# A gated layer of 32 experts: the next chunk's first two products stand between a chunk's turns and its second products, and tokens are gathered token-major two chunks ahead

## What is computed

```python
def moe_ffn(h, w_router, b_router, w1, b1, w2, b2):
    logits = (hf @ w_router + b_router).astype(jnp.float32)
    top_v, top_e = lax.top_k(logits, TOP_K)          # 4 of 32
    gates = jax.nn.softmax(top_v, axis=-1)
    ...
    def expert_block(args):
        xi, e = args
        hc = xi @ w1[e] + b1[e]                       # 1024 -> 2048
        g, u = hc[:, :D_EXPERT], hc[:, D_EXPERT:]
        g = jnp.minimum(g, SWIGLU_LIMIT)
        u = jnp.clip(u, -SWIGLU_LIMIT, SWIGLU_LIMIT)
        hm = (u + 1.0) * (g * jax.nn.sigmoid(SWIGLU_ALPHA * g))
        return hm @ w2[e] + b2[e]                     # 1024 -> 1024
```

## Time and profile before

| | us |
|---|---|
| median of 3 runs (2340.43 to 2341.96) | 2341.57 |
| the profiled execution | 2340.47 |
| its span, first to last instruction | 2338.7 |
| TensorE matmul busy | 2244.8 (96%) |
| VectorE busy | 714.5 (31%) |
| ScalarE busy | 620.8 (27%) |
| bytes moved | 688.71 MB, mean 294 GB/s |

### The profile page before, as it was taken

One profiled execution on the slowest core, in us unless ns is written; L12 is line 12 of the kernel. 1 busy time (PEld: TensorE's weight loads), 2 busy tenths in 40 slices (PEclk: granted clock), 3 DMA queues, 4 the chain that ended last, 5 costly groups with the idle time before them and its releaser, 6 DMA issues.

```text
span 2338.7 us, 36205 instructions
## 1 busy us (share of the span) xinstructions
PE 2244.8 (96%) x13812; PEld 1373.0 (59%) x13813; DVE 714.5 (31%) x1376; ACT 620.8 (27%) x903; POOL 394.1 (17%) x371
## 2 busy tenths in 40 slices
PE   7999999999999999999998999999999999999898
PEld 5887744444444444444446988899998863333333
DVE  4864322222222222222225244312315341111013
ACT  2143111111111111112124671443458011111111
POOL 2000000000000000000003761688586000000000
PEclk9999999999999999999999999999999999999999
DMA  9973399999999999989994533555454475999652
GB/s 359 381 259 110 101 411 418 418 418 418 418 418 418 417 418 418 418 363 380 418 418 167 179 109 108 180 183 180 127 180 117 155 287 216 402 405 396 276 230 84
DMA packets 223487, 688.71 MB, mean 294 GB/s; under 512 B 28330, under 2 KB 117362, under 8 KB 187570
## 3 DMA queue, kind: packets, MB, share of 16 engines
q1 hardware_dynamic: 221776, 685.82, 76.4%
q10 hardware_dynamic: 1490, 1.61, 0.2%
q0 software_dynamic: 144, 0.20, 0.0%
HBM read 686.53 MB, written 1.05 MB: 294 GB/s over the span
## 4 chain that ended last, share of the span: by engine, by line
PE 72%; DMA 11%; SPq 11%; DVE 3%; issue 2%; ACT 1%; POOL 0%; ACTq 0%; DVEq 0%; POOLq 0%
PE PS L1102 17%; PE PS L702 12%; DMA RAW<-in_w_exp_in 10%; PE PS L691 6%; SPq L467 6%; PE PS L1206 6%; PE PS L676 6%; PE PS L1066 4%; PE PS L1217 3%; SPq L489 3%; PE PS L1407 3%; PE PS L1085 2%; PE PS L748 1%; PE PS L1113 1%; SPq L497 1%
## 5 line engine op out<-in xcount | busy, mean ns | idle before, releaser
L1102 PE MATMUL PS<-RAW,Z 128*64 128x512 f32 x3168 | 713.3, 597 | 24.1 <-DMA RAW<-in_w_exp_in 23.2
L409 POOL TENSOR_TENSOR WLO_D<-W,WHI_D 128x512 fp32r<-128x512 f32 x284 | 360.2, 1304 | 1159.6 <-ACT SPARE L1632 965.9
L1102 PEld LDWEIGHTS PS<-RAW,Z 128*64 128x64 f32 x3168 | 213.7, 136 | 454.7 <-issue 376.8
L1206 PE MATMUL PS<-W,Z 128*64 128x512 f32 (+1 forms) x1056 | 212.5, 558 | 10.9 <-DMA W<-in_moe_w 10.2
L702 PE MATMUL PS<-Z,W 128*128 128x256 f32 x768 | 170.1, 382 | 1.5 <-DVE Z L2072 1.5
L405 ACT ACTIVATE WHI_D<-W 128x2048 fp32r<-128x2048 f32 x71 | 135.3, 1908 | 114.0 <-DMA W<-in_ffn_w 42.3
L1206 PEld LDWEIGHTS PS<-W,Z 128*64 128x64 f32 x1056 | 74.5, 137 | 148.9 <-issue 129.6
L702 PEld LDWEIGHTS PS<-Z,W 128*128 128x128 f32 x768 | 146.4, 191 | 23.0 <-DVE Z L2072 1.9
L1066 PE MATMUL PS<-Z 128*128 128x64 f32 x1088 | 125.3, 273 | 0.0
L1066 PEld LDWEIGHTS PS<-Z 128*128 128x128 f32 x1088 | 124.2, 192 | 0.2 <-issue 0.2
L2194 DVE TENSOR_TENSOR Z<-Z,PS 128x1024 f32<-128x1024 f32 x66 | 80.4, 1218 | 126.0 <-PE PS L1085 126.0
(11 more groups left out here) (405 smaller groups left out, 2692.8 us busy)
## 6 DMA issues: line engine op xcount, KB each, us to landing
RAW<-in_w_exp_in SPq DMA_DIRECT2D x256, 1024.0 KB, 19.2
RAW<-in_w_exp_out SPq DMA_DIRECT2D x128, 1024.0 KB, 21.7
W<-in_moe_w SPq DMA_DIRECT2D x128, 704.0 KB, 15.7
W<-in_w_in SPq DMA_DIRECT2D x52, 1024.0 KB, 5.4
W<-in_moe_w SPq DMA_DIRECT2D x40, 1024.0 KB, 15.9
W<-in_ffn_w SPq DMA_DIRECT2D x33, 1024.0 KB, 5.3
W<-in_w_ada SPq DMA_DIRECT2D x24, 1024.0 KB, 14.2
W<-in_w_out SPq DMA_DIRECT2D x12, 1024.0 KB, 5.0
```

Source lines behind the costliest of these rows:

```text
L409: i = eng.tensor_tensor(lo[:, c:c + 512], raw[:, c:c + 512], hi[:, c:c + 512].bitcast(F32), ALU.subtract)
L1102: mm = pe.matmul(ps(bank, 512, 64 * h, 64 * h + 64), x, w[:, c:c + 512], start=first, stop=final, skip_group_check=True)
L1206: mm = pe.matmul(o if b < 2 else o.rearrange("p (i n) -> p i n", i=2), X1[:, s, :], rhs, start=(s == 0), stop=(s == 7), skip_group_check=True)
```

## The change

- The next chunk's products 0 and 1 (`lead(g + 1)`) are issued after `turn_hidden(g)`, where the gather stood; the first chunk's are issued ahead of the loop. They count on a semaphore of their own, `m1_lead_done`, so that SP waits for it for groups 0 and 1 and for `m1_group_done` (now ten per chunk) for the rest.
- The gather is token-major, as in the second layer, and one chunk earlier in time than before: `gather(g + 3, 4)` stands between `scatter(g, 1)` and products 10 and 11 and writes bank 4. ACT copies it to XH2 (`tokens_major`), TensorE turns it in the next chunk after product 7 (`turn_x(g + 2)`, bank 2), and ACT copies that to X1.
- Ahead of the loop there are now two gathers, one turn and the first two products. DVE makes the second pick after its copy into Y.
- The last chunk stands outside the loop, without `turn_x`, `lead` and `gather`.

```diff
--- before.py
+++ after.py
@@ -477,10 +477,13 @@
                 with sp.Fori(0, 31) as before:
                     final = sp.value_load(TAB[0:1, bass.ds(before + ENDS, 1)], min_val=0, max_val=47)
                     for s in range(12):
-                        sp.wait_ge(sem("m1_group_done"), final * 12 + (s + 1))
+                        if s < 2:
+                            sp.wait_ge(sem("m1_lead_done"), final * 2 + (s + 1))
+                        else:
+                            sp.wait_ge(sem("m1_group_done"), final * 10 + (s - 1))
                         sp.nop(nofuse=True)
                         group(s, before + 1)
-                sp.wait_ge(sem("m1_group_done"), last * 12 + 12)
+                sp.wait_ge(sem("m1_group_done"), last * 10 + 10)
 
             def experts2():
 
@@ -1058,14 +1061,22 @@
 
             def experts1():
 
-                def gather(g1):
+                def gather(g1, bank=3):
 
                     pe.wait_ge(sem("m1_pick"), g1)
-                    for k in range(KT):
+                    for h in range(2):
                         for a in range(2):
-                            mm = pe.matmul(ps(2, HALF, c0=k * HALF), HT[:, a, k * P:(k + 1) * P], PICK[:, a, 0:HALF],
-                                           start=(a == 0), stop=(a == 1))
+                            mm = pe.matmul(ps(bank, 512, 64 * h, 64 * h + 64), PICK[:, a, 0:HALF], HT[:, a, 512 * h:512 * (h + 1)],
+                                           start=(a == 0), stop=(a == 1), skip_group_check=True)
                     mm.then_inc(sem("m1_gathered"), 1)
+
+                def turn_x(g1):
+
+                    pe.wait_ge(sem("m1_xh_copied"), g1)
+                    pe.nop(nofuse=True)
+                    for j in range(4):
+                        tr = pe.transpose(ps(2, P, c0=j * P), XH2[:, j * P:(j + 1) * P], IDENT[:, :])
+                    tr.then_inc(sem("m1_x_turned"), 1)
 
                 def turn(g):
 
@@ -1101,7 +1112,7 @@
                             c = i * 1024 + h * 512
                             mm = pe.matmul(ps(bank, 512, 64 * h, 64 * h + 64), x, w[:, c:c + 512], start=first, stop=final,
                                            skip_group_check=True)
-                    mm.then_inc(sem("m1_group_done"), 1)
+                    mm.then_inc(sem("m1_lead_done" if s < 2 else "m1_group_done"), 1)
 
                 def turn_hidden(g):
 
@@ -1114,28 +1125,44 @@
                         tr.then_inc(sem("m1_hidden_turned"), 1)
 
 
-                count = route(m1, H, WR1, gather)
-                with pe.Fori(0, count) as g:
+                def lead(g):
+
                     e = pe.value_load(TAB[0:1, bass.ds(g, 1)], min_val=0, max_val=31)
                     pe.wait_ge(sem("m1_x_copied"), g + 1)
                     for s in range(2):
                         product(g, e, s)
+
+                def chunk(g, more):
+                    e = pe.value_load(TAB[0:1, bass.ds(g, 1)], min_val=0, max_val=31)
                     turn(g)
                     for s in range(2, 8):
                         product(g, e, s)
 
                     pe.wait_ge(sem("m1_turned_copied"), g + 1)
+                    if more:
+                        turn_x(g + 2)
                     pe.wait_ge(sem("m1_ys_copied"), g + 1)
                     scatter(g, 0)
                     turn_hidden(g)
-                    gather(g + 2)
+                    if more:
+                        lead(g + 1)
                     pe.wait_ge(sem("m1_hm"), g + 1)
                     for s in range(8, 10):
                         product(g, e, s)
                     scatter(g, 1)
+                    if more:
+                        gather(g + 3, 4)
                     for s in range(10, 12):
                         product(g, e, s)
-                pe.wait_ge(sem("m1_x_copied"), count + 1)
+
+                count = route(m1, H, WR1, lambda g1: gather(g1, 0))
+                turn_x(1)
+                gather(2)
+                lead(0)
+                last = pe.value_load(TAB[0:1, LAST:LAST + 1], min_val=31, max_val=47)
+                with pe.Fori(0, last) as g:
+                    chunk(g, True)
+                chunk(last, False)
                 turn(count)
                 pe.wait_ge(sem("m1_turned_copied"), count + 1)
                 pe.wait_ge(sem("m1_ys_copied"), count + 1)
@@ -1620,9 +1647,15 @@
 
                 def tokens(g1):
 
+                    act.wait_ge(sem("m1_x_turned"), g1)
+                    act.activation(X1H, ps(2).rearrange("p (j h c) -> p j h c", j=4, h=2), ACT.Copy).then_inc(sem("m1_x_copied"), 1)
+
+                def tokens_major(g1, bank):
+
                     act.wait_ge(sem("m1_gathered"), g1)
-                    act.activation(X1, ps(2).rearrange("p (k c) -> p k c", k=KT), ACT.Copy).then_inc(sem("m1_x_copied"), 1)
-
+                    act.activation(XH2, ps(bank), ACT.Copy).then_inc(sem("m1_xh_copied"), 1)
+
+                tokens_major(1, 0)
                 tokens(1)
                 act.wait_ge(sem("route_tables"), 1)
                 count = act.value_load(TAB[0:1, COUNT:COUNT + 1], min_val=32, max_val=48)
@@ -1631,22 +1664,27 @@
 
                     act.activation(SPARE[:, q + 1:q + 2], ONES[:, 0:1], ACT.Copy).then_inc(sem("m1_split_room"), 1)
 
+                tokens_major(2, 3)
+
                 def chunk(g, split=None):
                     turned(g)
                     if split:
-                        act.wait_ge(sem("m1_group_done"), g * 12 + 2)
+                        act.wait_ge(sem("m1_lead_done"), g * 2 + 2)
                         split()
-                        act.wait_ge(sem("m1_group_done"), g * 12 + 6)
+                        act.wait_ge(sem("m1_group_done"), g * 10 + 4)
                         room(0)
-                    act.wait_ge(sem("m1_group_done"), g * 12 + 8)
+                    act.wait_ge(sem("m1_group_done"), g * 10 + 6)
                     act.activation(HS1[:, 0:512], ps(0), ACT.Copy).then_inc(sem("m1_hs_act"), 1)
+                    if not split:
+                        tokens(g + 2)
                     act.wait_ge(sem("m1_gate_part"), g + 1)
                     act.activation(SIG1, GPART, ACT.Sigmoid, scale=1.702).then_inc(sem("m1_sig"), 1)
-                    tokens(g + 2)
                     if split:
                         act.wait_ge(sem("m1_hm"), g + 1)
                         room(1)
-                    act.wait_ge(sem("m1_group_done"), g * 12 + 12)
+                    else:
+                        tokens_major(g + 3, 4)
+                    act.wait_ge(sem("m1_group_done"), g * 10 + 10)
                     act.activation(YS1, ps(3), ACT.Copy).then_inc(sem("m1_ys_copied"), 1)
 
                 last = act.value_load(TAB[0:1, LAST:LAST + 1], min_val=31, max_val=47)
@@ -2205,6 +2243,9 @@
                     return ps(b).rearrange("p (j a c) -> p j a c", j=4, a=2)
 
                 count = route(m1, R_BR1, lambda: pick(0, 0))
+                e1, c1 = chunk_of(1)
+                dve.wait_ge(sem("m1_gathered"), 1)
+                pick(e1, c1)
                 dve.wait_ge(sem("m1_added"), 1)
                 mch = Chain(dve, sem("m1_dve_step"))
                 with dve.Fori(0, count) as g:
@@ -2213,10 +2254,10 @@
                     dve.wait_ge(sem("m1_turned"), g + 1)
                     pick_gated(e, c)
                     mch.link(dve.tensor_copy(B1C, VEC[:, bass.ds(e * 16 + V_B1, 16)]))
-                    e1, c1 = chunk_of(g + 1)
-                    dve.wait_ge(sem("m1_gathered"), g + 1)
+                    e1, c1 = chunk_of(g + 2)
+                    dve.wait_ge(sem("m1_gathered"), g + 2)
                     pick(e1, c1)
-                    dve.wait_ge(sem("m1_group_done"), g * 12 + 8)
+                    dve.wait_ge(sem("m1_group_done"), g * 10 + 6)
                     dve.tensor_copy(HS1[:, 512:1024], ps(1)).then_inc(sem("m1_hs_dve"), 1)
 
                     dve.wait_ge(sem("m1_hidden_turned"), g * 2 + 1)
```

## The result

The changed kernel takes 2353.6 us (median of 4 runs, 2351.54 to 2356.26); the kernel before, run again beside it, 2341.0 (2339.14 to 2341.96). The ratio is 1.0057, with a 95% interval of 1.0044 to 1.0069: slower by 0.57%. The forecast was 2353.7.

A forecast was written before the change was run, and what follows sets the result against it. The prediction took the weight stream, at 417 to 418 GB/s, to bound the stage. Its terms, +2.9 + 2.0 + 6.5 - 1.4 + 2.1 = +12.1 us, gave 2353.7 us from the median 2341.57; 8-in-10 range 2345 to 2361.

The forecast's parts named there:

- The stream is the ceiling, TensorE's saving counts for nothing: Experts' loop: weights stream at 30.12 us per expert, so a chunk of 26.87 us instead of 28.08 gains nothing.
- some 485 us of busy time from 500 to 1044: Sign in the long window: TensorE's busy time falls from 520.7, with 3.25 us idle per expert over 18 experts.
- The two-chunk expert, +6.5 less 1.4: Expert 25: stream gaps sum to 17.55 us against 11.0, +6.5; today's weak restart is taken off, -1.4.
- 5.7 + 8.7: First and second gaps in the stream at the two-chunk expert, in us, before groups 0 and 2 of expert 26.
- 1.8 + 1.35: Third and fourth gaps in the stream at the two-chunk expert, in us, before groups 8 and 10 of expert 26.
- The two small gaps in chunk 0, +2.0: First chunk: groups 8 and 10 flow at 24.6 and 31.0 against 23.9 and 29.7; +2.0 us.
- The start, +2.9: Ahead of the loop: first product starts at 289.2 to 290.9, middle 290.0, instead of 287.11; +2.9 us.
- the lower bound, 1.6 us better than the upper one: Start: second pick at 287.3 if its register loads run under DVE's copy, 288.9 if they follow it.
- the rival of the clock at the start: TensorE, nearly idle before the second gather, drops its clock for the first products; +2 to +5 us, chance 0.12.
- The register load, 0.3: Expert-number load before the two moved products: between 0 and 0.83 us, taken as 0.3.
- The tail, +2.1: Last chunk: nothing covers the HM wait, so TensorE ends 12.75 us after the stream instead of 10.7; +2.1.
- The clock at every expert (0.08): Rival, chance 0.08: waits of about 2.4 us drop the clock, costing at the two-chunk expert and tail; 2359 to 2364 us.

The follow-up runs named there:

- run 6: Also extra_work: the changed kernel with two more 512-column matmuls on ones in every chunk, ahead of the hidden turns; 2363.91 us, ratio 1.0088.
- Run 2: The changed kernel with groups 0 and 1 of each expert issued by GpSimd on its own queue; 2341.68 us, ratio 1.0000 to before.
- runs 4 and 5: The kernel before and the changed kernel, each leaving out one expert's tokens beyond 64, so no expert has two chunks; 2323.28 and 2334.67 us.
- no_lead: The changed kernel with products 0 and 1 back at the head of their own chunk; 2446.02 us, ratio 1.0447.
- start_lead_first: The changed kernel with the first chunk's two products ahead of the second gather, before the loop; 2348.34 us, ratio to before 1.0030.
- queue_start_tail: The changed kernel with GpSimd's queue for groups 0 and 1, first products before the second gather, three last-chunk matmuls on ones; 2335.16 us, ratio 0.9978.

## Why the prediction was right, step by step

- **The stream is the ceiling, TensorE's saving counts for nothing.** Right: 418 GB/s in both kernels, and run 6 puts 63 us of work into the slack for some 6. The chunk is 26.87 us as worked out. The forecast of some 485 us of busy time from 500 to 1044 was too low, 500.2 were measured: idle time is 2.43 us per expert, not 3.25. Part of the slack was spent at a lower clock (below).
- **The two-chunk expert, +6.5 less 1.4.** Right in how the stream breaks, and in size. The holes have the forecast's pattern: 14.8 us of flow missing from 1044 to 1075 against 5.7 + 8.7 = 14.4, and 20 x (417 - 349) / 417 = 3.3 from 1080 to 1100 against 1.8 + 1.35. Over 1040 to 1100 the rate is 291 GB/s and was 329: 60 x 38 / 418 = +5.5, for a forecast of +5.1. Run 2, in which both holes shrink, and run 6, which rules the waits out, show the cause to be the one queue. What the sum got wrong is what the holes are worth at the end: it took before's tail of 10.7 us as given, but 3.1 of that is the same expert's doing. Without a second chunk the two kernels are 13.1 us apart and with it 14.0, so the expert's own part in the loss is 0.9, not 5.
- **The two small gaps in chunk 0, +2.0.** Measured: the stream's difference of 7.5 less 5.5 leaves 2.0, and the pair of runs 4 and 5, without the two-chunk expert, gives 2.0.
- **The start, +2.9.** Measured +3.5, by another way. DVE's copy ends at 284.56 (282.27 and 2.29 long) and the pick starts at 284.48, so its register loads ran under the copy: the lower bound, 1.6 us better than the upper one. But the second gather took 3.14 us instead of 1.87, and the first products 3.94 instead of 3.65: the rival of the clock at the start did occur (0.12), at 1.6 us in place of the 2 to 5 that I gave it. Two misses cancelled; the middle of the range was right by luck as much as by reason. Where the clock held under the same order (extra_work, no_lead), the start is 9.6 and 9.8, +1.8 and +2.0 against before.
- **The register load, 0.3.** Measured 0: no gap inside the 7.02 us step. The lower bound held.
- **The tail, +2.1.** Measured +3.0. The wait for HM came as forecast; that the clock falls in it and adds 1.77 us (5.35 for 3.58) I had only in a rival. Without that the tail would be 11.9, not the 12.75 worked out: products 2 to 7 end 1.8 us ahead of the stream's end and not 1.07, and product 8 starts 4.34 behind the hidden turns and not 4.54. So here too a term that was too large stands beside one that was missing. Runs 4 and 5 show besides that the +3.0 is a net of two things that I had not told apart: a backlog that before carries and the new order doesn't, and an idle wait and a clock that only the new order has.
- **The clock at every expert (0.08).** It half happened. From 360 to 932 product 0 waited 20 times. 12 of these waits were 2.3 to 2.4 us long, and behind 7 of the 12 the four products took 8.6 to 8.9 us instead of 7.0; behind the other 5, and behind the 8 shorter ones (0.74 to 1.69), nothing changed. The slack paid for it: the wait after a fall was 1.4 to 1.7 us. In the window of the two-chunk expert the clock was 1.00, so the 2359 to 2364 didn't come. The Trainium skill (TensorE: Matmul & The Clock Gate, Part 1) has a kernel whose clock fell on the wait of every tile, and gives these waits as some 3 to 5 us. The waits here are shorter, 2.4 us at most, so the prediction read too much into that page when it made this rival its result; the clock fell on 7 waits in 20.
- The sum of the forecast was 12.1. In the layer it was 3.5 + 7.5 + 3.0 = 14.0, in the medians 12.6. The terms of the stream carry the forecast; 3.4 of the 14.0 are time at the lower clock, for which the sum had nothing, and terms that were too large, by some 1.0 us at the start and 0.8 in the tail, took part of it up. That the median lands within 0.1 us of the forecast is luck. The gap between the last two is within what the untouched parts vary by, and I can't divide it further.

What stays open: why some waits of 2.4 us bring the lower clock and others, as long, don't; why in no_lead it lasts longer in every other chunk; and how much E - G varies from one execution of a kernel to the next, since each was profiled once.

## What to carry to other kernels

Where one queue issues refills in a fixed order, moving the use of a buffer moves its release. Ask for every release whether it still comes in the order of issue in the odd case (here an expert with two chunks); a release that comes early is worth something only on a queue where nothing late stands ahead of it.
Where the stream is the ceiling, saved work becomes idle time, and what is left to win or lose lies at the start, at breaks of the stream, and in the tail: take E minus G apart into these three before arguing about the middle.
An edit that takes cover away from a wait is priced twice where nothing has slack: the wait, and the lower clock behind it.

## What the runs showed of the hardware

- **The clock behind waits.** In after, waits of TensorE of 2.4 us for a landing were followed by 0.50 in some cases (8.88 us for 32 matmuls, else 7.02) and not in others; the waits of 3.3 us in no_lead were followed by 5.24 and 6.37 us for 16 instead of 3.58, in turn; the waits of 0.56 us in before never showed it. By the rows at either level one fall costs 1.6 to 1.9 us behind a wait of 2.4 in after, and 1.4 to 3.1 behind one of 3.3 (5.01 us in start_lead_first, 6.63 in extra_work). It reached the end where nothing has slack: at the start, behind the stream's last landings, and in every chunk of no_lead.
- **Useless matmuls as a cover.** Two matmuls on ones per chunk made the products 13 us shorter in sum (708.0 for 721.1), and three in the wait for HM of queue_start_tail's last chunk brought products 8 and 9 to 3.65 us from 5.35. Where they stand matters: the two of extra_work stand ahead of the hidden turns, TensorE then waits 3.3 us in its last chunk as before, and products 8 and 9 take 6.63.
- **GpSimd's queue** carried 64 transfers of 1 MB inside the same plateau of 418 GB/s, with a median of 9.4 us from issue to landing where those of `w_exp_in` by SyncE in the same kernel took 23.1. By these medians they don't stand behind SyncE's own.
